# Where the split hidden activations and the sliding heads' split output start in on-chip memory

## The reference

```python
def swiglu(h, w_in, w_out):
    a, b = jnp.split(h @ w_in, 2, axis=-1)
    return (jax.nn.silu(a) * b) @ w_out          # w_in 1024 x 5632, w_out 2816 x 1024, twice

# second block
y = jnp.concatenate([ya, yb], axis=-1) @ w_out_even[i]   # ya retention, yb sliding window; 2048 x 1024
x = x + y
h = rms_norm_2(x, norm_mlp[layer])
x = x + jnp.square(jax.nn.relu(h @ w_mlp_up[layer])) @ w_mlp_down[layer]   # 1024 x 4096, 4096 x 1024
```

## The kernel before

| tiles | start modulo 256, before | after the change |
|---|---|---|
| `raw`, `whi`, `wlo` | 128 | 128 |
| `x`, `hhi`, `hlo` (behind `skew`, 192 bytes) | 64 | 64 |
| `ada_ring`, `acc_a`, `xn1`, `xn2`, `f1`, `f2`, `f3r`, `tok3` and others | 32 | 32 |
| `tmp1`, `hid1`, `acc_b`, `hidhi1`, `hidlo1` (behind `skew1`) | 64 | 128 |
| `tmp2`, `hid2`, `hidhi2`, `hidlo2` (behind `skew2`) | 64 | 128 |
| `sbias`, `prob3`, `pt3` | 192 | 192 |
| `yhi3`, `ylo3`, `qkhi`, `nsink` | 192 | 128 |

## Time and profile before

### The profile page before, as it was taken

How to read it: one execution, slowest core, us unless ns; L and a number is a source line. 1 busy time by engine, 2 the same in 40 slices (tenths; PEclk the granted TensorE clock), 3 DMA queues, 4 the chain that set the end, 5 groups by cost and what they waited for, 6 DMA issues and landing times.

```text
span 1327.7 us, 22440 instructions
## 1 busy us (share of the span) xinstructions
PE 1310.5 (99%) x8876; PEld 1186.1 (89%) x8876; DVE 869.6 (65%) x1140; ACT 721.1 (54%) x1070; POOL 49.6 (4%) x76
## 2 busy tenths in 40 slices
PE   8999999999999999999999999999999999999999
PEld 7998899999899779999989899889999888899997
DVE  6889878885898556555565675565555577655554
ACT  3676544444644556444466663655555667655554
POOL 0101000000111000000001000000000000000000
PEclk8899899999999999999999999999999999999999
DMA  9977789985799623555546544355655543455540
GB/s 353 368 283 266 263 284 320 321 304 194 248 355 352 209 68 127 191 190 190 191 157 212 173 134 134 127 184 191 192 191 191 186 160 100 132 192 190 190 158 33
DMA packets 147361, 275.54 MB, mean 208 GB/s; under 512 B 4727, under 2 KB 85391, under 8 KB 147160
## 3 DMA queue, kind: packets, MB, share of 16 engines
q1 hardware_dynamic: 132176, 220.21, 49.3%
q0 software_dynamic: 13872, 52.05, 11.5%
q10 hardware_dynamic: 1240, 2.26, 0.5%
HBM read 273.40 MB, written 1.10 MB: 207 GB/s over the span
## 4 chain that ended last, share of the span: by engine, by line
PE 91%; DVE 4%; ACT 2%; issue 1%; DMA 1%; ACTq 0%; DVEq 0%
PE ps L1986 89%; PE ps L2127 1%; DVE acc_a L1224 1%; DVE wlo L1211 1%; PE ps L2363 1%; ACT whi L514 1%; DMA voh<-in_voh 1%; DMA ada_ring<-in_ada_w 0%; ACT xn L568 0%; DVE x L1312 0%; DVE xn L1325 0%; DVE h L1304 0%; PE ps L2471 0%; DVE x L1319 0%; ACT small L575 0%
## 5 line engine op out<-in xcount | busy, mean ns | idle before, releaser
L1211 DVE TENSOR_TENSOR wlo<-raw,whi 128x1024 fp32r<-128x1024 f32 x400 | 484.7, 1223 | 343.0 <-ACT whi L514 342.7
L514 ACT CAST whi<-raw 128x1024 fp32r<-128x1024 f32 x400 | 418.7, 1053 | 462.0 <-PE ps L1986 450.6
L1986 PE MATMUL ps<-hhi,whi 128*128 128x256 f32 x1792 | 504.3, 281 | 2.5 <-DVE hlo L1372 2.0
L1986 PE MATMUL ps<-hlo,whi 128*128 128x256 f32 x1792 | 497.6, 278 | 0.0
L1986 PE MATMUL ps<-hhi,wlo 128*128 128x256 f32 x1792 | 497.4, 278 | 0.0
L1986 PEld LDWEIGHTS ps<-hhi,whi 128*128 128x128 f32 x1792 | 337.0, 188 | 9.5 <-issue 6.4
L1986 PEld LDWEIGHTS ps<-hlo,whi 128*128 128x128 f32 x1792 | 337.9, 189 | 4.4 <-issue 2.2
L1986 PEld LDWEIGHTS ps<-hhi,wlo 128*128 128x128 f32 x1792 | 336.7, 188 | 0.0
L1986 PE MATMUL ps<-whi,hidlo 128*128 128x512 f32 x432 | 170.2, 394 | 0.0
L1986 PE MATMUL ps<-wlo,hidhi 128*128 128x512 f32 x432 | 169.4, 392 | 0.0
L1986 PE MATMUL ps<-whi,hidhi 128*128 128x512 f32 x432 | 168.3, 390 | 0.0
(11 more groups left out here) (238 smaller groups left out, 1162.1 us busy)
## 6 DMA issues: line engine op xcount, KB each, us to landing
raw<-in_ffn_w_in SPq DMA_DIRECT2D x44, 1024.0 KB, 6.1
ada_ring<-in_ada_w POOLq DMA_DIRECT2D x40, 1024.0 KB, 7.5
raw<-in_w_mlp_up SPq DMA_DIRECT2D x32, 1024.0 KB, 5.4
raw<-in_w_mlp_down SPq DMA_DIRECT2D x32, 1024.0 KB, 5.0
raw<-in_ffn_w_out SPq DMA_DIRECT2D x22, 1024.0 KB, 5.0
raw<-in_att_w_qkv SPq DMA_DIRECT2D x18, 1024.0 KB, 6.0
raw<-in_w_in_even SPq DMA_DIRECT2D x18, 1024.0 KB, 5.1
raw<-in_hyb_w_in SPq DMA_DIRECT2D x10, 1024.0 KB, 11.0
```

The source lines that it names most:

```text
L514: A.copy(whi[:, H % 4, :], raw[:, slot(n), h * HALF:(h + 1) * HALF]).then_inc(s["hi_ready"], 1)
L1211: V.tensor_tensor(wlo[:, H % 4, :], raw[:, slot(n), h * HALF:(h + 1) * HALF], whi[:, H % 4, :].bitcast(F32), ALU.subtract).then_inc(s["lo_ ...
L1986: return pe.matmul(out, lhsT, rhs, start=first, stop=last, skip_group_check=True)
```

## The change

Three fillers: two grow from 32 to 96 bytes per partition, and a third of 192 bytes is put ahead of `yhi3`. The starts that follow are in the table above. No instruction is added, removed or moved on any engine, no wait changes, and no operand changes its shape or step.

```diff
@@ -127,7 +127,7 @@
             with ExitStack() as r:
-                sb(r, "skew1", [P, 8])
+                sb(r, "skew1", [P, 24])
                 tmp1 = sb(r, "tmp1", [P, 2, 512])
                 hid1 = sb(r, "hid1", [P, 2, 512])
                 acc_b = sb(r, "acc_b", [P, 2 * 512])
@@ -154,7 +154,7 @@
         with ExitStack() as r:
-            sb(r, "skew2", [P, 8])
+            sb(r, "skew2", [P, 24])
             tmp2 = sb(r, "tmp2", [P, 3, 512])
             hid2 = sb(r, "hid2", [P, 3, 512])
             hidhi2 = sb(r, "hidhi2", [P, 3, 512], F32R)
@@ -179,6 +179,7 @@
             prob3 = sb(r, "prob3", [P, 3, 512])
             pt3 = sb(r, "pt3", [P, 2, 512])
+            sb(r, "skew3", [P, 48])
             yhi3 = sb(r, "yhi3", [P, 8, S], F32R)
             ylo3 = sb(r, "ylo3", [P, 8, S], F32R)
             qkhi = sb(r, "qkhi", [P, 5, 512], F32R)
```

## The result

The changed kernel takes 1335.99 us (median of 12 runs, 1333.1 to 1338.98) against 1330.89 for the kernel before on the same chips; the ratio is 1.004, 95% interval 1.0027 to 1.0054. It is slower by 0.4%, where 0.5% faster was forecast.

A forecast was written before the change was run, and what follows sets the result against it. TensorE was taken as the bound, so savings per matmul show almost one for one. Faster downs (5.5 us), first downs (0.4), `yhi3` (0.85) and `hhi` (0.4), together 7.2 us, gave 1322.3 profiled, 1321 median; range 1309 to 1337.

The forecast's parts named there:

- What bounds the kernel, and that starts act at all: TensorE, in flight 99% of the span, is the bound; start addresses change the distance between its matmuls.
- The two beats: TensorE's matmuls: steady distances 4.4 ns apart, 229 and 233 ns at 512 columns, 113.3 and 117.8 in the ups.
- The downs' beat: 52 ordinary feed-forward downs, 1248 matmuls, go from 228.9 to 224.5 ns each: 5.5 us less.
- below 228: Downs in the profile after: the prediction is wrong if their distance per matmul isn't below 228 ns.
- The neighbours: Stretches behind moved ones inherit a beat: `hhi` behind `yhi3` saves 0.4 us; ups stay at 113.3 ns.
- The slow rival: Downs on the slow beat, 5.5 us more (0.20); with the ups behind them slow too, 14.4 us more (0.14).
- The sign of being wrong: Downs below 228 ns but the end not following: TensorE waits for weights, ScalarE's 450.6 us wait shrinks by far more.
- The range: Whole kernel, 1309 to 1337 us; leaves out slow downs with slow ups and the edge of nearly all loss gone.
- The scores as evidence: Attention scores: stationary and moving tiles said to start equal, 118 ns a matmul, the slow beat; cited for the slower rival.
- The page's rule: TensorE never waits on anyone and weight loads steal no bandwidth, so the change is worth 0, leaving 1328 us.
- What two reads meeting would make of it: Downs and `yhi3`: moving read and weight load meet at equal places modulo 256, each meeting costs; equal starts save 4.4 ns.

The follow-up runs named there:

- half_last: The changed kernel with the last three matmuls of each down made as six of 256 columns; 1325.98 us, ratio 0.9966 to the kernel before; repeated: 1325.93 us, 0.999.
- h_128: The changed kernel with `hhi` and `hlo` also starting at 128 modulo 256; 1351.24 us, ratio 1.0162 to the kernel before.
- unread_only: The kernel before with only the feed-forward tiles that TensorE doesn't read in the downs moved to 128; 1329.88 us, ratio 1.0009.

## Why the prediction was wrong

- *What bounds the kernel, and that starts act at all*: right. TensorE waits for nothing new, and every experiment that moved tiles which TensorE reads changed its beats. The two beats and their 4.4 ns were read rightly. That a run keeps the beat it was begun with holds within one form in most stretches; across forms it doesn't: behind slow ups downs at 64 came on 233.3 or on 229, and in `half_last` the output projection behind a slow query projection was on 228.9.
- *The downs' beat*, the term "from 228.9 to 224.5": right in sign, half in size, and the mark "below 228" was met. It was 226.7, so 1248 x 2.2 = 2.7 us in place of 5.5. The size was an extrapolation in steps of 4.4; 2.2 is half a step. With the first downs, `yhi3` and the `hhi` behind it the terms of the sum came to 4.0 us in place of 7.2. Equal starts were the best pair for this form, in the downs, in `yhi3` (226.6 where 224.5 was said) and in the projections of `h_128`.
- *The neighbours*: this is the step that failed. The sum had no term for the ups behind the downs ("Ups: 113.3 as before"), although the text had found that runs inherit their beat. They went to 117.8, all 3072, 12.5 us, three times what the listed terms gave back. The evidence that I used against it was one hand-over: the first down of the kernel before, on 233.3, was followed by fast ups. But a down's new beat is a new hand-over, and what the old one led to says nothing of it. The runs showed these maps: at 64 a beat leads to itself, but not where the down itself stays on 233.3, as in the earlier trace rows; at 128 every down leads to slow ups, at 192 to the other beat, and at 128 with a changed last matmul to ups on 113.3.
- *The slow rival* had nearly the right price, 14.4 us for the ups, but tied it to slow downs and put it at 0.14. Its mark, "ordinary downs read above 231 ns", was wrong: they read 226.7 and the kernel was slower. It also counted 20 x 96 + 28 x 48 = 3264 matmuls; a SwiGLU has nine pairs of ups behind a down, not ten, so 18 x 96 + 28 x 48 = 3072.
- *The sign of being wrong* that the prediction gave for a fast down and a slow end, that TensorE began to wait for weights, was a wrong alternative: ScalarE still waited 444.1 us for TensorE (450.6 before), and the time went into TensorE's own ups.
- *The range*: 1335.99 lies within 1309 to 1337, but there it stood for slow downs. That it fits is luck.
- *The scores as evidence* were misread. The code takes the hi parts of queries and keys from `qkhi` and the lo parts from `f3r`. So only two of a head's six matmuls, those of hi by hi, have equal starts (192 with 192); the other four pair 192 with 32, and none has 32 with 32. Their 118 ns therefore said nothing of equal starts, neither against the downs nor for the 120.0 that the ups of `h_128` showed later. The price of nothing for them was right: over the 16 heads they changed by 0.1 us.
- *The page's rule* (the Trainium skill, "SBUF — State Buffer", "Who interferes with whom": TensorE waits on no one; "TensorE: Matmul & The Clock Gate", Part 2, step 1: the next weight load takes no bandwidth from the running matmul) would have the change worth 0, and it wasn't: at one clock and one shape the 256-column matmuls ran at 113.3 to 120.0 ns and the 512-column ones at 226.7 to 233.3 by the starts and the hand-over alone. Whether it is the weight load that the running matmul meets, no run shows.
- *What two reads meeting would make of it*: the sketch of meetings gave the order 128, 64, 192 for the downs, and that order came out (226.7, 228.9, 233.3). It gave nothing for the ups and nothing for the maps, and a start of 0 in place of 64 made the projections slower (232 to 234 ns), where the sketch has the first meeting come later still. Why the beats are what they are was not settled; only that they hang on the starts and the hand-over.

## What to carry to other kernels

Where TensorE runs without a pause, price a change of layout by the distance of starts in the timeline, over every form of matmul and every hand-over between them: a stretch that gains 2 ns a matmul can leave the next one, with twice as many, 4 ns worse. A mean duration or a busy share shows little of it: the ups' records went from 278 to 279 ns, TensorE's share stayed at 99%. And before a layout is judged, try another last matmul at the hand-over, which costs little: at 128 one more matmul in each of some 50 downs took 11.0 us (0.8%) off the changed kernel. It has to be tried at each layout, since a like edit at 64 cost 0.5%.

## What the runs showed of the hardware that was not expected

- A stretch of matmuls falls into a beat that repeats exactly: in 512 columns mostly 226.7, 228.9 or 233.3 ns, in 256 columns 113.3, 117.8 or 120.0 (118.3 to 118.8 at two of the starts), within six matmuls of its begin, and can hold it for hundreds (575 in the earlier trace rows). It can also change on the way, beside a single longer distance: in `half_last_again` the query projection made 384 matmuls at 113.3, then one distance of 133 ns, and the other 192 at 117.8.
- Two of these beats can both be steady at the same addresses (113.3 and 117.8 at 128 and 64), and the choice is carried through a stretch of another form with the same mean: in `unread_only` downs of 229 ns handed on slow to slow, in the kernel before fast to fast. What differs is the place in the round of 226, 229 and 232 ns at which the down ends.
- The plain float32 matmuls ran at 215.4 ns for 256 columns and no layout tried brought a split one of 512 columns there; 226.7 was the best.
